# A two-block transformer on one core: convolution inputs, row differences and transposes issued earlier in the mixed block, and three weight remainders on DVE instead of POOL in the differential attention

## The reference, cut to what matters

```python
def _diff_attention(xn, w_in, q_gain, k_gain, lam, subln, w_out, lam_init):
    q, k, v = jnp.split(xn @ w_in, 3, axis=-1)        # 8 heads, two maps each
    ...
        p = jax.nn.softmax(s + bias[None, :, None], axis=-1)
        a = p[:, :, 0] - lmbda * p[:, :, 1]
        return jnp.einsum('bhqk,bhkd->bhqd', a.astype(v.dtype), v)
    ...
    o = _rms(o, subln) * (1.0 - lam_init)
    return o.reshape(B, T, H * 2 * Dh).astype(xn.dtype) @ w_out

# the mixed layer of the second block
    proj = u @ w_in[layer]
    aq, ak, av, dqkv, dgate, da, db = jnp.split(proj, SPLITS, axis=-1)
    o_att = chunked_rel_attention(...)
    dqkv = causal_short_conv(dqkv, dn_conv_w[layer])   # 4 taps along time, then silu
    log_decay = -jnp.exp(dn_a_log) * jax.nn.softplus(da + dn_dt_bias)
    beta = jax.nn.sigmoid(db)
    o_dn = gated_delta_rule(dq, dk, dv, log_decay, beta)
# in gated_delta_rule, chunks of 64
    diff = decay[..., :, None] - decay[..., None, :]
    l_mask = jnp.where(tril, jnp.exp(jnp.where(tril, diff, 0.0)), 0.0)
    a_strict = jnp.where(strict, jnp.einsum('bhnid,bhnjd->bhnij', k_beta, k) * l_mask, 0.0)
    # (I + a_strict) is inverted, then the chunks are run through one after another
```

## Time and profile before

| what | value |
| --- | --- |
| three runs | 1440.24, 1440.28 and 1437.13 us, median 1440.24 |
| the profiled execution | 1439.79 us, of which the span is 1438.0 |
| PE busy | 1418.0 us, 99% of the span |
| DVE, ACT, POOL busy | 892.8, 732.2 and 113.7 us |
| mean granted TensorE clock | 0.998 |
| bytes moved | 248.86 MB, mean 173 GB/s |

### The profile page before, as it was taken

One profiled execution on the slowest core, in us unless ns is written; L12 is line 12 of the kernel. 1 busy time (PEld: TensorE's weight loads), 2 busy tenths in 40 slices (PEclk: granted clock), 3 DMA queues, 4 the chain that ended last, 5 costly groups with the idle time before them and its releaser, 6 DMA issues.

```text
span 1438.0 us, 21399 instructions
## 1 busy us (share of the span) xinstructions
PE 1418.0 (99%) x7875; PEld 1194.6 (83%) x7875; DVE 892.8 (62%) x1076; ACT 732.2 (51%) x954; POOL 113.7 (8%) x111
## 2 busy tenths in 40 slices
PE   9999999999999999999999999999999989999999
PEld 8888888768888888888888778888888778888887
DVE  5666665866666676666644455766664776576564
ACT  6545465656454564544544444545455755354442
POOL 0000013440000000000000210000000142000000
PEclk9999999999999999999999999999999999999999
DMA  7655655326565555656654545655566312155552
GB/s 250 228 179 189 221 180 176 118 89 205 182 198 175 178 191 186 198 182 199 226 183 149 176 139 169 203 182 186 193 204 215 120 57 90 59 202 179 193 191 85
DMA packets 156459, 248.86 MB, mean 173 GB/s; under 512 B 9728, under 2 KB 101488, under 8 KB 156144
## 3 DMA queue, kind: packets, MB, share of 16 engines
q1 hardware_dynamic: 153728, 243.54, 51.9%
q10 hardware_dynamic: 2672, 4.51, 0.9%
HBM read 246.97 MB, written 1.05 MB: 172 GB/s over the span
## 4 chain that ended last, share of the span: by engine, by line
PE 92%; DVE 4%; ACT 2%; issue 1%; DMA 0%; ACTq 0%; POOL 0%; DVEq 0%
PE bank L1914 27%; PE bank L1843 15%; PE bank L1844 15%; PE bank L1845 15%; PE bank L1920 14%; PE bank L1860 1%; DVE w_lo L1252 1%; PE bank L2296 1%; ACT w_hi L572 1%; ACT room L742 1%; PE bank L2228 0%; DVE recip_lam L1424 0%; DVE kT L1606 0%; PE bank L1963 0%; DVE room L1292 0%
## 5 line engine op out<-in xcount | busy, mean ns | idle before, releaser
L1252 DVE TENSOR_TENSOR w_lo<-raw,w_hi 128x2048 fp32r<-128x2048 f32 x225 | 515.1, 2292 | 346.9 <-ACT w_hi L572 346.6
L572 ACT ACTIVATE w_hi<-raw 128x2048 fp32r<-128x2048 f32 x228 | 434.6, 1909 | 219.5 <-PE bank L1920 134.4
L1914 PE MATMUL bank<-xT,w_hi 128*128 128x512 f32 x1648 | 450.0, 394 | 0.5 <-DVE xT L1312 0.4
L1914 PEld LDWEIGHTS bank<-xT,w_hi 128*128 128x128 f32 x1648 | 284.8, 189 | 44.1 <-DVE xT L1312 2.7
L1920 PEld LDWEIGHTS bank<-xT,w_lo 128*128 128x128 f32 x1648 | 245.0, 188 | 29.9
L1920 PE MATMUL bank<-xT,w_lo 128*128 128x256 f32 x1648 | 253.9, 281 | 0.0
L1843 PE MATMUL bank<-w_hi,xT 128*128 128x512 f32 x508 | 203.7, 401 | 0.2 <-DVE xT L1803 0.2
L1845 PE MATMUL bank<-w_hi,xT 128*128 128x512 f32 x508 | 198.3, 390 | 0.0
L1844 PE MATMUL bank<-w_lo,xT 128*128 128x512 f32 x508 | 197.9, 390 | 0.0
L1845 PE MATMUL bank<-w_hi,hT_lo 128*128 128x512 f32 x500 | 194.6, 389 | 0.0
L1843 PE MATMUL bank<-w_hi,hT_hi 128*128 128x512 f32 x496 | 193.9, 391 | 0.0
(11 more groups left out here) (311 smaller groups left out, 1049.7 us busy)
## 6 DMA issues: line engine op xcount, KB each, us to landing
raw<-in_ffn_w_in SPq DMA_DIRECT2D x174, 512.0 KB, 4.7
raw<-in_ffn_w_out SPq DMA_DIRECT2D x88, 512.0 KB, 4.2
raw<-in_w_ff SPq DMA_DIRECT2D x64, 512.0 KB, 4.2
raw<-in_rt_w_in SPq DMA_DIRECT2D x48, 512.0 KB, 4.6
raw<-in_w_in SPq DMA_DIRECT2D x28, 512.0 KB, 4.8
raw<-in_da_w_in SPq DMA_DIRECT2D x24, 512.0 KB, 4.6
raw<-in_rt_w_out SPq DMA_DIRECT2D x16, 512.0 KB, 4.1
raw<-in_da_w_out SPq DMA_DIRECT2D x8, 512.0 KB, 4.2
```

The source lines that it names most:

```text
L572: act.activation(w_hi[:, n % RING, :], raw[:, n % RING, :], ACT.Copy).then_inc(hi_ready, 1)
L1252: dve.tensor_tensor(w_lo[:, n % RING, :], raw[:, n % RING, :], w_hi[:, n % RING, :].bitcast(F32), ALU.subtract).then_inc(lo_ready, 1)
L1914: return pe.matmul(dst[:, :], hi[:, k, cols], flat(xT[:, 4 * j + k, :, :]), start=j == 0 and k == 0, stop=j == 1 and k == 3)
```

## The change

It has two parts. In the mixed layer:

- ACT's copies `take_conv(0)` and `take_conv(2)` stand ahead of the exponentials and the logarithm of the decay, no longer behind them and a `split`. DVE's copies `take_conv(1)` and `take_conv(3)` stand ahead of `log_decay` and of the remainder of block `n0 + 9`.
- On PE the wait for `proj_read` at m = 4, 5 and 6 stands directly ahead of the block's matmuls, behind the transposes and row products of that chunk.
- On DVE the row differences (with the difference for `etail`) stand ahead of `att_sum_squares(1)` and the remainder of block `n0 + 12`.
- On DVE `maxima(1)` stands behind the first inverse (`mx_inv0`), and `level_mask(1)` ahead of the wait for `mx_N0T`.

In the differential attention the three remainders leave POOL. DVE makes those of `n1 + 2` and `n1 + 3` in halves of 128x1024, one half at the end of each turn `i` = 5 to 8, and that of `n1 + 4` whole, behind the loop.

```diff
@@ act, mix
                 act.activation(conv_w[:, :], bank[7][:, 0:48], ACT.Copy).then_inc(mx_convw, 1)
+                act.wait_ge(mx_zero, 1)
+                take_conv(0)
+                take_conv(2)
                 act.wait_ge(mx_convw, 1)
...
                 split(n0 + 9)
-                act.wait_ge(mx_zero, 1)
-                take_conv(0)
-                take_conv(2)
                 read(3)
@@ pool, da
                 for h in range(3, DA_H):
                     head_norm(h)
-                    if h in (3, 5, 7):
-                        split(first["da_out"] + (h - 3) // 2 + 2)
@@ dve, da
+                def split_part(n, part):
+                    dve.wait_ge(hi_ready, n + 1)
+                    at = slice(part * D, part * D + D)
+                    ins = dve.tensor_tensor(w_lo[:, n % RING, at], raw[:, n % RING, at], w_hi[:, n % RING, at].bitcast(F32),
+                                            ALU.subtract)
+                    if part:
+                        ins.then_inc(lo_ready, 1)
...
                     if i <= DA_H + 1:
                         head_normed(i - 2)
-                dve.wait_ge(lo_ready, RING + n1 + 5)
+                    if 5 <= i <= DA_H:
+                        split_part(n1 + 2 + (i - 5) // 2, (i - 5) % 2)
+                split(n1 + 4)
@@ dve, mix
                 split(n0 + 8)
+                take_conv(1)
+                take_conv(3)
                 log_decay()
                 split(n0 + 9)
-                take_conv(1)
-                take_conv(3)
                 split(n0 + 10)
...
                 att_sum_squares(0)
-                att_sum_squares(1)
-                split(n0 + 12)
                 dve.wait_ge(mx_dec, 1)
...
                 dve.tensor_scalar(flat(dn_LT), flat(dn_LT), 0.0, None, ALU.min).then_inc(mx_diff, 1)
+                att_sum_squares(1)
+                split(n0 + 12)
                 convolve(2)
...
                 maxima(0)
-                maxima(1)
...
                 link(dve.tensor_tensor(dn_XT, own_idents, dn_X, ALU.subtract))
+                level_mask(1)
                 dve.wait_ge(mx_N0T, 1)
                 dve.tensor_tensor(dn_X, own_idents, by_pair(bank[5][:, :]), ALU.subtract).then_inc(mx_inv0, 1)
-                level_mask(1)
+                maxima(1)
@@ pe, mix
                     for j in range(2):
-                        if j == 0:
-                            pe.wait_ge(proj_read, 6 + 2 * (18 + (m if m > 3 else max(m - 2, 0))))
+                        if j == 0 and m <= 3:
+                            pe.wait_ge(proj_read, 6 + 2 * (18 + max(m - 2, 0)))
...
+                        if j == 0 and m > 3:
+                            pe.wait_ge(proj_read, 6 + 2 * (18 + m))
                         in_block(n0 + 2 * m + j, j, mx_pair[m] * 2, norm=6 if m == 0 else None, done=proj_done)
```

5 lines of the change are left out of this document (removed).

## The result

After the change the kernel takes 1430.15 us (median of five executions: 1429.75, 1429.99, 1430.15, 1430.22 and 1434.00). Before it takes 1439.42 (five beside them, 1437.13 to 1440.28). The ratio is 0.9946 with a 95% interval of 0.9932 to 0.9961. That is 9.3 us faster. The prediction said 1433.9, with a range from 1430.5 to 1437.2. The time lies 3.75 under the forecast and 0.35 under the range, and within 1.1 of the rival *no drop of the clock* (1431.2).

The account below looks back on a forecast made before the run. PE, busy 1418.0 of 1438.0 us, bounds the kernel, so only its waits and low clock can yield. 2.6 + 3.7 = 6.3 off 1439.79 gives 1433.5, plus 0.45 for the median: 1433.9, range 1430.5 to 1437.2.

Parts of the forecast that it names:

- no drop of the clock: Rival: the low-clock stretch in level 1 does not come, another 2.76 us less, 1431.2; chance 0.24.
- Differential attention, 2.6: Turns of heads 5 and 7: PE's waits behind DVE instructions held by POOL go, 2.6 us, bounds 1.5 and 2.8.
- The cover named for the halves: Ahead of mix_maps DVE idles 1.12 us; each half of 1.22 stands there and sticks out by 0.10.
- Mixed layer, projection: PE's lead over its old times grows from 1.7 at m = 4 to 4.9 to 5.0 us at to_tokens(1).
- Mixed layer, behind the projection, 3.7: DVE and POOL decide here; of PE's lead 3.7 us stays to the end, bounds 1.3 and 5.0.
- gain of DVE's chain at the product that the turned tokens need: Behind the projection, DVE's list wins only its 1.15 wait and small change, 1.27 us.
- new wait at the second half of the turned tokens: At L2441 PE arrives at 1170.0, DVE's product ends at 1171.9: a wait of 1.9 us, lead down to 3.1.
- new wait at the pair scores: pair_scores needs DVE's two kT instructions of 0.75 each: a wait of 0.6 us, lead down to 2.5.
- DVE's chain holds everything: Rival: behind the projection DVE and POOL bind PE, the mixed layer gains only 1.3 us, 1436.3; chance 0.15.
- The clock, 0 for a gain of 2.76: PE's clock still falls once, in level 1 or a little earlier, costing about the same, so no gain was counted.
- two low stretches: Rival: the clock falls at the new wait of 1.9 and is still low in level 1, 1436.2; chance 0.10.
- slower: the low clock stays: Rival: the level loop's small matmuls don't bring the clock back, 2.76 us per level, up to 1444.5; chance 0.04.

Follow-up runs that it names:

- experiment 7: Kernel after, with the remainders of n1 + 2 and n1 + 3 made whole on DVE at the end of turns 6 and 8, not in halves: 1431.21 us.
- experiment 11: Kernel after, with the four copies of the convolution inputs (DVE's and ACT's) put back to their old places: 1430.57 us.
- experiment 9: Kernel after, with POOL's two products over the tokens behind the second inverse and its next three steps one level later each: 1430.18 us.
- experiment 5: Kernel after, with PE's proj_read waits of m = 4, 5 and 6 put back ahead of the transposes: 1431.56 us.
- experiment 4: Kernel after, with maxima(1) and level_mask(1) put back to their old places: 1430.58 us.
- experiment 1: Kernel before, with the differential attention's part of the change alone: 1434.76 us.
- experiment 3: Kernel before, with 14 and 7 unread 64x64 matmuls in PE's two waits ahead of level 1: 1436.89 us.
- experiments 2, 5 and 7 to 11: Before with the mixed layer's part alone (1433.61 us), and edits of after, including DVE's second sum of squares first (1430.45), also with POOL's products later (ratio 0.9938).
- experiment 6: Kernel after, with the second sum of squares and the remainder of n0 + 12 put back ahead of the row differences: 1434.63 us.

## Why the prediction was right and where it was wrong

**What bounds the kernel.** Right: only PE's waits and PE's clock moved the time. DVE carries 2.7 us more, and in the attention no PE wait comes of it.

**Differential attention, 2.6.** Right: 2.74 in after, 2.82 alone. The cover named for the halves (DVE's idle time ahead of `mix_maps`) holds; experiment 7 shows that it was wider than I said.

**Mixed layer, projection.** The leads foretold were 1.7, 2.0, 3.9 and 4.9 to 5.0. From the starts of the rows, less the 3.58 that lie ahead of the layer, they are 1.78 (1128.38 and 1123.02), 1.82 (1141.39 and 1135.99), 3.69 (1152.13 and 1144.86) and 4.69 (1159.47 and 1151.20). The last two were put 0.2 too high, and the 0.2 is already in the second. The short wait for the decay's copy was put at about 0.4 and is 0.41. By experiment 11 the first of these, 1.7, is worth nothing at the end.

**Mixed layer, behind the projection, 3.7.** The mechanism was right and the sizes nearly so:

| step | forecast | measured |
| --- | --- | --- |
| gain of DVE's chain at the product that the turned tokens need (1171.94 and 1167.07) | 1.27 | 1.29 |
| new wait at the second half of the turned tokens | 1.9 | 1.33 |
| new wait at the pair scores | 0.6 | 0.32 |
| wait at the inverse's transposes | 1.0 | 1.29 |
| wait ahead of level 1 | 0.4 | 0.52 |
| lead at level 1 | 3.7 | 3.45 |

The first new wait is smaller because PE comes 0.3 later than foretold and because its idle time is counted behind the drain. The one at the inverse's transposes is 0.3 larger by two small errors: PE gets there with a lead of 2.65, not 2.5 (1180.56 - 1.63 and 1173.99 - 1.29, less 3.58), and DVE's product, held by POOL, ends with one of 2.99, not 3.1. In experiment 9, with POOL silent, that wait is 0.65. The rival *DVE's chain holds everything* was half right. DVE and POOL do hold the lead at level 1 to 3.0 to 3.6 us, whatever PE has won before (3.45 in after, 3.04 in experiment 5, 3.58 in experiment 11). But more than the 1.3 of DVE's list is kept, as the prediction had reasoned: PE has its own transposes in between.

**The clock, 0 for a gain of 2.76. This is the step that failed:** "I take it that PE's clock falls once, here or a little earlier". The price held (2.76, read from the trace of before; 2.8 between the medians of its two groups, 3.0 in experiment 4, 4.2 in experiment 1), and the guess that the run of 1437.13 was one without that stretch fits the lower group (1435.84 to 1437.87). What was wrong was to take the fall as a fixed event that moves. Whether it comes changes from one execution to the next: 32 of 52 executions of before are at 0.998 or less, and of the five of after one has it clearly (1434.00; another, at 0.998 too, lies at 1430.22 and pays nothing that I can name). I added two new waits of 1.9 and 0.6 and held them for as bad as the old ones of 1.63 and 0.98. But the clock stays at 1.00 behind them in the trace of after. Experiment 3 shows the pair of waits ahead of level 1 as the cause in before: filled, the mean is 0.999 or 1.000 in ten of ten. That the fall is rarer in the new order is shown by counting: of the 44 executions of after and of experiments 2, 5 and 7 to 11 (without the one of 5023 us), which all have the new order of the masks and of the row differences, 9 are at 0.998 or less, against 32 of 52 of before (a split as uneven by chance has odds under 1 in 10000). Why it is rarer is argued, not shown. The pair shrank from 2.61 to 1.81, but experiment 4, with 2.28 left, had two of five, too few to tell. That the new waits do no harm because they stand behind 128 x 128 transposes isn't shown either: experiment 6 has a fall at a longer wait, of 3.70, between large matmuls and such transposes.

The rivals *two low stretches* and *slower: the low clock stays* priced the same step the other way. In the trace of after they did not come: it has no low stretch between 4.80 and 1428.15 us. That the time lies so near to *no drop of the clock* is in part luck, as the next paragraph shows.

**The median.** The forecast went from one profiled execution of before to the median, and so carried two things of that execution through: the low clock in level 1, and the slow start, which the prediction didn't see. Of the 3.75 by which the forecast is too high, 2.76 is the clock, 0.84 is what before's trace was behind at the first wait of the attention, and the two parts of the change were put 0.11 too high (6.3, and 2.74 + 3.45 = 6.19), which lessens it. The rest, 0.29, is how the medians lie to the profiled executions: 0.45 above in the prediction, 0.16 above in after. That is the sum for two traces. How the start is spread over the other executions no trace shows.

The Trainium skill says (TensorE: Matmul & The Clock Gate, What's actually happening) that the throttled state is the default and that activity releases it. The runs agree: the fall comes at waits of PE, and filled with matmuls these bring none at 0.998 or less in ten executions (experiment 3). But they don't bear out the use I made of it, that any new wait counts: those of 1.33 and 0.32 brought no low stretch in the trace of after.

## What to carry to other kernels

Read the waits of the engine that bounds the kernel up to the last place at which it waits for others. What it wins ahead of that place is worth only as much as the others' chain wins too: here a lead of 1.7 us was worth nothing, one edit carried two thirds of the layer's gain, and the chain's pace was set by POOL and DVE holding each other, not by DVE's list alone. Before a gain is put against a median, look whether the executions fall in two groups by granted clock, since an edit may change which group holds the median: a third of this gain (2.8 of 9.3 us) is that. The start of a program can differ between executions too, so compare traces from a point behind it. And work moved to an engine that stands idle isn't free if it holds another: three remainders of 4.6 us on POOL cost the attention 2.7 us of PE's time, and on DVE next to nothing.

## What the runs showed of the hardware

- The clock also falls among the large matmuls of a projection: behind a wait of 3.70, eight 128 x 128 transposes took 1.97 instead of 1.04, and the stretch from 1148 to 1152 has a granted clock of 0.50 (experiment 6).
- At the start of the program the row of the granted clock doesn't tell all. In before the stretch below stands at 1.00, while the eight transposes in it take 1.97, as those at a granted 0.50 do in experiment 6, and 1.09 in after. The trace's record of the clock has its first entry at 11.77 in before, behind this stretch, and at 4.80 in after:

```profile
4.00:8.00 4.00, 2.92 (x17) 2.37 (x16) 0.69 (x3) 2.07 (x5) 0.00 (x0) 1.00 1.00 333
```

- The hold goes both ways. POOL's square of 128x512 takes 4.73 us beside the last convolution products of DVE, a remainder of 2.29 and a small product, which leave DVE no pause, and 1.04 when DVE is idle (POOL's timeline of after):

```profile
1149.39 4.73 POOL L1173 TENSOR_TENSOR relu<-room 128x512 f32<-128x512 f32 x1
1154.99 1.04 POOL L1173 TENSOR_TENSOR relu<-room 128x512 f32<-128x512 f32 x1 [0.87 <-DVE small L1612]
```
